# Selected attention: score products of the next unit issued in twos between the steps of a weight chunk

## The chip, the cores and the metric

The kernel runs on one core of one Trainium2 chip. The metric is the device time of one execution in microseconds; the kernel before takes 2013.05 us, the median of three runs (2012.48 to 2014.12).

## The reference, cut to what matters

The program is two transformer blocks on 512 tokens of width 1024, in float32. The first has a gated feed-forward, a windowed attention with a pooling branch and a second feed-forward. The second projects its input to the parts of a sparse attention (compressed keys, selected blocks, a window), of an RWKV-7 recurrence and of two gates, and ends with a convolutional feed-forward. The change touches the sparse attention:

```python
s_c = jnp.einsum('bsgrd,bcgd->bgrsc', q, kc).astype(jnp.float32) + bias_c
p_c = masked_softmax(s_c, dist_c >= 0, axis=-1)
o_cmp = jnp.einsum('bgrsc,bcgd->bsgrd', p_c, vc)
...
sc = jnp.einsum('bcgrd,bgcnld->bgrcnl', q_b, k_sel).astype(jnp.float32) + bias
p = masked_softmax(sc, mask, axis=(-2, -1))
...
o = gt[..., 0:1] * o_cmp + gt[..., 1:2] * o_slc + gt[..., 2:3] * o_win
```

There are 8 heads of width 64 in 2 groups of 4, and with 8 blocks of 64 keys every causal block is among the 16 selected, so selected and window attention are both causal attention over the keys up to the query, on keys of their own.

## The kernel before

The five engines each run a list of instructions written out by hand, joined by semaphores. All large weights come as one stream of chunks (128 x 1024 numbers). SP loads a chunk into one of 4 places of `w_raw`; POOL splits it into a high and a low float32r part (`split`, L445 and L447) when the chunk four earlier has been used (`w_used`); TensorE multiplies it. `chunk` (L521) does a chunk in 8 steps `k`, three 128x512 products each: `h_hi` by `w_hi` (L532), `h_lo` by `w_hi` (L533), `h_hi` by `w_lo` (L534), 24 in all, into one bank of PSUM.

The sparse attention is cut in 8 units (`units`): query tiles of 128 tokens, n = 0 to 3, by the two groups g. Unit 0 and 1 have n = 0, 2 and 3 n = 1, and so on. For a unit:

- TensorE, `nsa_scores` (L838): 10 score products into four banks in turn. Products 0 to 7 (L847) are one head each against the (n + 1) x 128 keys, on 64 rows of the array: even ones on rows 0 to 63, odd ones on rows 64 to 127. Products 8 and 9 (L854) are two heads each against the 8n + 7 compressed keys, again on one half of the rows each. Product i may overwrite its bank only when DVE has read product i - 4 (`nsa_masked`).
- DVE, `nsa_mask`: adds the bias to each product, writes it to `E` (L2000; `Ec`, L2008, for 8 and 9) and takes the minimum.
- ACT, `nsa_exps`: the exponential of each (L1458; for 8 and 9 two each, L1464), each with a read of its accumulator.
- DVE, `nsa_weights`: scales them by gate over sum (L2024 to L2036), then `nsa_weighed`.
- TensorE, `nsa_weigh` (L862): turns the weights 128 columns at a time (L880), ACT copies each turned item to `p2T` (L1479), TensorE multiplies it by the values (L894). Turned item x + 1 is issued ahead of the product of item x. ACT then copies the result to `oA` (L1483).

Between these, TensorE works through chunks of the RWKV and gate projections (`fill`, L759), one per unit; while the units run these go to bank 7, and ACT copies each to `stage` (L1404) when the chunk is used and sends it to memory (L1380). The orders of the three engines are, in TensorE's code,

```python
nsa_scores(*units[0], 0)
fill()
for u, (n, g) in enumerate(units):
    if u + 1 < len(units):
        nsa_scores(*units[u + 1], u + 1)
    fill()
    nsa_weigh(n, g, u)
```

on ACT `nsa_exps` of unit u + 1, then the copy of the chunk (`fill_out`), then the `p2T` copies of unit u; and on DVE `nsa_weights` of unit u, then `nsa_mask` of unit u + 1. All three work through their lists strictly in that order.

Of the kernel before, what the change touches and what calls it, by code (L numbers as in the profile page):

```python
# [115 lines left out]
def build(nc, x, positions, params, const, mix_const, w_pool, w_ffn1_gu, w_ffn1_down, w_in, w_out, w_ffn2_gu,  # L116
          w_ffn2_down, w_nsa, nsa_const, rel_bias, distance_code, cmp_pe, cmp_w1, cmp_w2,
          w_rwkv, rwkv_const, rwkv_w2a2, rwkv_g2, w_gates, w_merge, w_out_2, w_conv_up, w_conv_down, out):
    with ExitStack() as ctx:
# [5 lines left out]
        def sem(name):  # L125

            name = SHARED.get(name, (name, 0))[0]
            if name not in sems:
                sems[name] = ctx.enter_context(nc.semaphore(name))
            return sems[name]  # L130

        def nth(name, count):

            return sem(name), count + SHARED.get(name, (name, 0))[1]
# [34 lines left out]
        bank = [psum[:, i, :] for i in range(8)]  # L169
# [90 lines left out]
        def fill_bank(f):  # L260

            return 4 + f % 4 if f < 14 else 7 if f < NFILL - LATE else (0, 1, 2, 4, 5, 3, 0)[f - NFILL + LATE]
# [12 lines left out]
        def half_rows(x):  # L275
            return slice(C * x, C * x + C)
# [242 lines left out]
        @block.tensor  # L519
        def _(pe):  # L520
            def chunk(c, s, k0, k1, rhs_hi, rhs_lo, dst, start, stop, each=None, w0=None, also=None,  # L521
                      shift=0):


                w0 = k0 if w0 is None else w0
                pe.wait_ge(*nth("w_split", c + 1))
                for k in range(k0, k1):
                    if each:
                        pe.wait_ge(*nth(each, k + 1 + shift))
                    hi = w_hi[:, s, (k - w0) * P:(k - w0 + 1) * P]  # L530
                    lo = w_lo[:, s, (k - w0) * P:(k - w0 + 1) * P]
                    nc.tensor.matmul(dst, hi, rhs_hi[:, k, :], start=start and k == k0, stop=False)  # L532
                    nc.tensor.matmul(dst, hi, rhs_lo[:, k, :], start=False, stop=False)  # L533
                    last = nc.tensor.matmul(dst, lo, rhs_hi[:, k, :], start=False, stop=stop and k == k1 - 1)  # L534
                    if also:
                        also(k)
                return last
# [21 lines left out]
            def ffn_down(tag, c0, read):  # L559

                def body(i, first):
                    for u in range(4):
                        if not first:
                            pe.wait_ge(*nth(read, 4 * i + u - 3))
                        for j, (a, b) in enumerate(DOWN_SPLIT):
                            v = 3 * u + j
                            if first and u == 0:
                                pe.wait_ge(*nth(tag + "_a_ready", b))
                            last = chunk(12 * i + (c0 + v), (c0 + v) % RING, a, b, a_hi, a_lo, bank[4 + u][:, :],
                                         j == 0, j == 2)  # L570
                            last.then_inc(sem("w_used"), 1)
                body(0, True)
                body(1, False)
# [66 lines left out]
            for n in range(NT):  # L640
                pe.wait_ge(*nth(f"x_in{n}", 16))
                for k in range(KD):
                    last = nc.tensor.transpose(bank[k][:, n * P:(n + 1) * P], x_tok[:, n, k * P:(k + 1) * P], ident)
# [43 lines left out]
            for n in range(NT):  # L687
                last = nc.tensor.transpose(bank[6][:, n * P:(n + 1) * P], z[:, 1, n * P:(n + 1) * P], ident)
# [5 lines left out]
            units = [(n, g) for n in range(NT) for g in range(2)]  # L694
# [61 lines left out]

            filled = [0]

            def fill(n=1):  # L759

                for f in range(filled[0], filled[0] + n):
                    if f == NFILL - 1:
                        pe.wait_ge(*nth("fill_read", NFILL - LATE + 1))
                    elif 4 <= f <= NFILL - LATE:
                        pe.wait_ge(*nth("fill_read", f - 3 if f < 14 else f))
                    chunk(FIRST["rwkv"] + f, (FIRST["rwkv"] + f) % RING, 0, KD, h_hi, h_lo,
                          bank[fill_bank(f)][:, :], True, True).then_inc(sem("w_used"), 1)
                filled[0] += n

            pe.wait_ge(*nth("zn_read", 11))  # L770
            for v in range(2):
                b = job_bank()
                for n in range(NT):
                    last = nc.tensor.transpose(b[:, n * P:(n + 1) * P], zn[:, 2 + v, n * P:(n + 1) * P], ident)
# [13 lines left out]
            for n in range(NT):  # L788
                last = nc.tensor.transpose(b[:, n * 24:(n + 1) * 24], oA[0:24, 0, n * P:(n + 1) * P],
                                           ident[0:24, 0:24])  # L790
# [14 lines left out]
            for v in range(2):  # L805
# [3 lines left out]
                for h in range(2):  # L809
                    for j in range(16):  # L810
                        last = nc.tensor.matmul(b[:, h * 64:h * 64 + 2 * NCMP], cw1[:, j, h * P:(h + 1) * P],  # L811
                                                cmp_blocks[v][:, j, :, :], start=(j == 0), stop=(j == 15),
                                                skip_group_check=True)
# [4 lines left out]
                if v == 0:  # L818
                    for h in range(2):
                        last = nc.tensor.matmul(b[:, 0:2 * NCMP], cw2[:, 0, h, :], hid[:, h, 0:2 * NCMP],  # L820
                                                start=(h == 0), stop=(h == 1))
# [5 lines left out]
                else:  # L827
                    for g in range(2):
                        for h in range(2):
                            last = nc.tensor.matmul(b[0:NCMP, g * HD:(g + 1) * HD], hid[:, h, g * NCMP:(g + 1) * NCMP],  # L830
                                                    cw2[:, 1, h, 0:HD], start=(h == 0), stop=(h == 1),
                                                    skip_group_check=True)
# [2 lines left out]
            pe.wait_ge(*nth("nsa_read", 17))  # L835
            pe.wait_ge(*nth("kc_normed", 1))

            def nsa_scores(n, g, unit):  # L838


                for i in range(10):
                    b = bank[i % 4] if unit % 2 == 0 else bank[(i + 2) % 4]
                    if 10 * unit + i >= 4:
                        pe.wait_ge(*nth("nsa_masked", 10 * unit + i - 3))
                    if i < 8:
                        h, e = i % 4, i % 2
                        last = nc.tensor.matmul(b[:, 0:(n + 1) * P],  # L847
                                                qn[64 * e:64 * e + 64, 2 * g + h // 2, n * P:(n + 1) * P],
                                                kd[64 * e:64 * e + 64, 2 * (i // 4) + g, 0:(n + 1) * P],
                                                start=True, stop=True)  # L850
                    else:
                        e = i - 8
                        for h in range(2):
                            last = nc.tensor.matmul(b[:, h * 32:h * 32 + 8 * n + 7],  # L854
                                                    qn[64 * e:64 * e + 64, 2 * g + h, n * P:(n + 1) * P],
                                                    kcn[64 * e:64 * e + 64, g * NCMP:g * NCMP + 8 * n + 7],
                                                    start=(h == 0), stop=(h == 1), skip_group_check=True)
                    last.then_inc(sem("nsa_scores"), 1)
# [45 lines left out]
                turn[0] += len(items)  # L904

            units = [(n, g) for n in range(NT) for g in range(2)]
            nsa_scores(*units[0], 0)
            fill()
            for u, (n, g) in enumerate(units):
                if u + 1 < len(units):  # L910
                    nsa_scores(*units[u + 1], u + 1)
                fill()
                nsa_weigh(n, g, u)


# [140 lines left out]
            for m in range(4):  # L1056
# [33 lines left out]
                for half in range(2):  # L1090
                    pe.wait_ge(*nth(f"dt_ready{half}", 6 * m + 6))
                    pe.wait_ge(*nth("rw_tok", 4 * m + 4))
                    for i in range(2):
                        n = 2 * half + i
                        for e, c in DIAGONALS:
                            rows = half_rows(e)
                            last = nc.tensor.matmul(bank[HALF_BANKS[half][e]][half_rows(c), i * P:i * P + P],
                                                    DT[rows, 2 * n + c, :],
                                                    AtV[rows, n, c, :, :].rearrange("p a i -> p (a i)"), start=True,
                                                    stop=True, skip_group_check=True)  # L1100
                    last.then_inc(sem("ug"), 1)
                pe.wait_ge(*nth("ug_read", 2 * m + 2))
                for n in range(NT):
# [18 lines left out]
                    for qm, yn, tok, rows, e, ug in tiles:  # L1122
                        last = nc.tensor.matmul(yn[:, second], Kt[tok, n, rows], Vt[tok, n, rows], start=False,
                                                stop=True, skip_group_check=True)
# [4 lines left out]
            for c in range(1, NCH):  # L1129
# [4 lines left out]
                for e in range(2):  # L1134
                    rows = slice(64 * e, 64 * e + 64)
                    if c < NCH - 1:
                        for m in range(4):
                            last = nc.tensor.matmul(bank[2 + e][rows, m * HD:(m + 1) * HD], pin[rows, 4 + m, at],
                                                    state[rows, c % 2, m, :], start=True, stop=True,
                                                    skip_group_check=True)  # L1140
                        last.then_inc(sem("state_product"), 1)
                for e in range(2):
                    rows = slice(64 * e, 64 * e + 64)
                    for m in range(4):
                        last = nc.tensor.matmul(bank[e][rows, m * HD:(m + 1) * HD], state[rows, c % 2, m, :],
                                                pin[rows, m, at], start=True, stop=True, skip_group_check=True)
# [48 lines left out]
            for n in range(NT):  # L1195
                for h in range(2):
                    for k in range(4):
                        last = nc.tensor.transpose(bank[2 * n + h][:, k * P:(k + 1) * P],
                                                   xT[:, 4 * h + k, n * P:(n + 1) * P], ident)
# [1193 lines left out]
```

## Time and profile before

| | us |
|---|---|
| median of three runs | 2013.05 |
| lowest, highest | 2012.48, 2014.12 |
| the profiled execution, its own time | 2012.64 |
| its span in the profile | 2010.8 |
| TensorE busy (matrix products) | 1863.6 |
| POOL busy | 1278.4 |
| DVE busy | 836.7 |
| ACT busy | 426.4 |
| mean granted TensorE clock | 0.965 of 2.4 GHz |

The profile is of one execution. "Busy" is the time in which an engine had an instruction under way. The span is 1.84 us shorter than that execution's own time, which also holds what lies around the instructions.

### The profile page before, as it was taken

The numbers are of one execution on the slowest core, as the hardware profiler recorded it, in microseconds if no ns is written. First come the engines' busy times: TensorE is split into PE (matmuls) and PEld (weight loads), VectorE is DVE, ScalarE is ACT, GpSimd is POOL, SyncE is SP. The second block draws the span as 40 slices with busy tenths as digits, with TensorE's granted clock in tenths as the row PEclk, the third lists the DMA queues.
The fourth block names the chain that finished last, engine by engine and source line by source line (L and its number), as shares of the span: only waits on it lengthen the run. The fifth ranks groups of instructions, "written<-read, shape, count | busy, mean of one in ns | idle before, by whom it ended". The sixth has DMA issues, their size and how long they took to land.

```text
span 2010.8 us, 29786 instructions
## 1 busy us (share of the span) xinstructions
PE 1863.6 (93%) x11700; PEld 1480.8 (74%) x11700; DVE 836.7 (42%) x1399; ACT 426.4 (21%) x862; POOL 1278.4 (64%) x619
## 2 busy tenths in 40 slices
PE   6999999888779999999799999998868799999998
PEld 5888888656557888888487876676755678888887
DVE  4333321268654333311405344327657635555301
ACT  3000000122422000000213255535431022111100
POOL 6888888734076888888475542323355567777773
PEclk9999999889889999999899999999968899999999
DMA  4222233311021222233242431140023223322331
GB/s 152 94 95 102 93 93 95 118 37 58 11 84 64 103 95 94 89 98 106 98 162 85 158 131 53 43 152 9 4 112 115 68 81 102 95 94 93 95 97 61
DMA packets 58779, 180.32 MB, mean 90 GB/s; under 512 B 6931, under 2 KB 13843, under 8 KB 58172
## 3 DMA queue, kind: packets, MB, share of 16 engines
q1 hardware_dynamic: 49132, 165.83, 24.7%
q10 hardware_dynamic: 9552, 13.13, 1.9%
q8 instruction: 72, 1.18, 0.2%
q14 instruction: 23, 0.19, 0.0%
HBM read 165.81 MB, written 13.13 MB: 89 GB/s over the span
## 4 chain that ended last, share of the span: by engine, by line
PE 81%; DVE 12%; ACT 3%; issue 2%; DMA 0%; POOL 0%; ACTq 0%; SPq 0%; DVEq 0%; POOLq 0%
PE bank L532 23%; PE bank L533 23%; PE bank L534 23%; PE bank L894 1%; PE bank L847 1%; DVE h_lo L1660 1%; PE bank L582 1%; PE bank L880 1%; DVE sq L2223 1%; DVE m_lo L2224 1%; PE bank L811 1%; DVE xT L1707 1%; DVE tmp L1704 1%; PE bank L1052 1%; DVE sq L2220 1%
## 5 line engine op out<-in xcount | busy, mean ns | idle before, releaser
L445 POOL TENSOR_TENSOR w_hi<-w_raw,one 128x1024 fp32r<-128x1024 f32 (+1 forms) x279 | 527.4, 1890 | 554.1 <-PE bank L534 543.6
L447 POOL TENSOR_TENSOR w_lo<-w_raw,w_hi 128x1024 fp32r<-128x1024 f32 (+1 forms) x279 | 695.9, 2494 | 21.9
L532 PE MATMUL bank<-h_hi,w_hi 128*128 128x512 f32 x1528 | 619.7, 406 | 26.9 <-DVE h_lo L1660 12.6
L533 PE MATMUL bank<-h_lo,w_hi 128*128 128x512 f32 x1528 | 598.4, 392 | 0.0
L534 PE MATMUL bank<-h_hi,w_lo 128*128 128x512 f32 x1528 | 598.1, 391 | 0.0
L532 PEld LDWEIGHTS bank<-h_hi,w_hi 128*128 128x128 f32 x1528 | 289.0, 189 | 111.3 <-issue 29.0
L533 PEld LDWEIGHTS bank<-h_lo,w_hi 128*128 128x128 f32 x1528 | 289.1, 189 | 67.2 <-issue 9.9
L534 PEld LDWEIGHTS bank<-h_hi,w_lo 128*128 128x128 f32 x1528 | 288.8, 189 | 61.0
L532 PE MATMUL bank<-a_hi,w_hi 128*128 128x512 f32 x528 | 205.4, 389 | 0.0
L533 PE MATMUL bank<-a_lo,w_hi 128*128 128x512 f32 x528 | 205.4, 389 | 0.0
L534 PE MATMUL bank<-a_hi,w_lo 128*128 128x512 f32 x528 | 205.4, 389 | 0.0
L1255 ACT ACTIVATE tmp<-tmp 128x512 f32<-128x512 f32 x44 | 27.8, 632 | 426.6 <-DVE tmp L1671 426.6
L1697 DVE TENSOR_TENSOR acc<-acc,sq 128x512 f32<-128x512 f32 x16 | 30.5, 1907 | 207.8 <-ACT sq L1264 207.8
L532 PEld LDWEIGHTS bank<-a_hi,w_hi 128*128 128x128 f32 x528 | 99.1, 188 | 20.7
L534 PEld LDWEIGHTS bank<-a_hi,w_lo 128*128 128x128 f32 x528 | 99.1, 188 | 20.6
L533 PEld LDWEIGHTS bank<-a_lo,w_hi 128*128 128x128 f32 x528 | 99.1, 188 | 20.4
L1671 DVE TENSOR_TENSOR tmp<-bank,rstd 128x512 f32<-128x512 f32 x44 | 30.4, 691 | 132.5 <-PE bank L534 123.9
L1679 DVE TENSOR_TENSOR a_hi<-tmp,bank 128x512 f32 x44 | 30.3, 688 | 132.2 <-PE bank L534 132.2
L493 POOL TENSOR_TENSOR OT<-mats,rcs 128x256 f32<-128x256 f32 x40 | 32.5, 825 | 75.0 <-DVE mats L2132 62.2
L1633 ACT ACTIVATE tmp<-bank,prm 128x512 f32<-128x512 f32 x44 | 34.3, 779 | 147.8 <-DVE bank L2246 147.8
L1674 DVE TENSOR_TENSOR tmp<-tmp,rstd 128x512 f32<-128x512 f32 x44 | 47.2, 1072 | 31.4 <-ACT tmp L1255 31.4
L1264 ACT ACTIVATE sq<-bank 128x512 f32<-128x512 f32 x16 | 9.6, 598 | 229.7 <-PE bank L534 229.7
(342 smaller groups left out, 2088.4 us busy)
## 6 DMA issues: line engine op xcount, KB each, us to landing
w_raw<-w_ffn_gu_dram SPq DMA_DIRECT2D x88, 512.0 KB, 3.4
w_raw<-w_conv_up_dram SPq DMA_DIRECT2D x44, 512.0 KB, 3.5
w_raw<-w_ffn_down_dram SPq DMA_DIRECT2D x32, 448.0 KB, 3.2
w_raw<-w_ffn_down_dram SPq DMA_DIRECT2D x16, 512.0 KB, 3.5
w_raw<-w_out_dram SPq DMA_DIRECT2D x16, 512.0 KB, 3.5
w_raw<-w_gates_dram SPq DMA_DIRECT2D x16, 512.0 KB, 3.6
w_raw<-w_rwkv_dram SPq DMA_DIRECT2D x14, 512.0 KB, 3.5
w_raw<-w_conv_down_dram SPq DMA_DIRECT2D x16, 448.0 KB, 3.3
```

What stands on the lines that cost most here:

```text
L445: nc.gpsimd.tensor_tensor(w_hi[:, s, 0:width], raw, one[:, 0:1].to_broadcast([P, width]), ALU.mult).then_inc(sem("w_rounded"), 1)
L447: nc.gpsimd.tensor_tensor(w_lo[:, s, 0:width], raw, w_hi[:, s, 0:width].bitcast(F32), ALU.subtract).then_inc(sem("w_split"), 1)
L493: nc.gpsimd.tensor_tensor(OT[:, k % 2, units_of(half), :] .rearrange("p (n e) t -> p n e t", e=2), mats[:, 2 * half:2 * half + 2, :, 0, :] ...
L532: nc.tensor.matmul(dst, hi, rhs_hi[:, k, :], start=start and k == k0, stop=False)
L533: nc.tensor.matmul(dst, hi, rhs_lo[:, k, :], start=False, stop=False)
L534: last = nc.tensor.matmul(dst, lo, rhs_hi[:, k, :], start=False, stop=stop and k == k1 - 1)
L1255: nc.scalar.activation(tmp[:, u, :], tmp[:, u, :], ACT.Silu).then_inc(sem(tag + "_silu"), 1)
L1633: nc.scalar.activation(tmp[:, v, :], bank[2 * u + v][:, :], ACT.Identity, bias=bias, scale=w)\
L1671: nc.vector.tensor_tensor(tmp[:, u, :], bank[2 * u][:, :], rstd[:, :], ALU.mult)\
L1674: nc.vector.tensor_tensor(tmp[:, u, :], tmp[:, u, :], rstd[:, :], ALU.mult)\
L1679: nc.vector.tensor_tensor(hi, tmp[:, u, :], bank[2 * u + 1][:, :], ALU.mult)\
L1697: nc.vector.tensor_tensor(acc[:, :], acc[:, :], sq[:, m % 2, :], ALU.add).then_inc(sem(tag + "_acc"), 1)
```

## The change

`chunk` gets the option to increment `w_used` itself at its last product, ahead of what hangs behind the step. `nsa_scores` takes the list of products to do. Of each of the units 1 to 7, products 0 and 1 now stand ahead of the chunk, and products 2 and 3, 4 and 5, 6 and 7, 8 and 9 behind the chunk's steps k = 1, 3, 5 and 7. Unit 0 keeps its ten products ahead of a chunk. DVE's, ACT's, POOL's and SP's lists are the same as before. In the changed file TensorE's lines from L535 on stand two lines lower (L847 is L849, L854 is L856, L880 is L882, L894 is L896).

```diff
             def chunk(c, s, k0, k1, rhs_hi, rhs_lo, dst, start, stop, each=None, w0=None, also=None,
-                      shift=0):
+                      shift=0, count=False):
...
                     last = nc.tensor.matmul(dst, lo, rhs_hi[:, k, :], start=False, stop=stop and k == k1 - 1)
+                    if count and k == k1 - 1:
+                        last.then_inc(sem("w_used"), 1)
                     if also:
                         also(k)
                 return last
...
-            def fill(n=1):
+            def fill(n=1, also=None):
...
                     chunk(FIRST["rwkv"] + f, (FIRST["rwkv"] + f) % RING, 0, KD, h_hi, h_lo,
-                          bank[fill_bank(f)][:, :], True, True).then_inc(sem("w_used"), 1)
+                          bank[fill_bank(f)][:, :], True, True, also=also, count=True)
...
-            def nsa_scores(n, g, unit):
+            def nsa_scores(n, g, unit, some):
...
-                for i in range(10):
+                for i in some:
...
-            nsa_scores(*units[0], 0)
+            nsa_scores(*units[0], 0, range(10))
             fill()
             for u, (n, g) in enumerate(units):
                 if u + 1 < len(units):
-                    nsa_scores(*units[u + 1], u + 1)
-                fill()
+
+                    nsa_scores(*units[u + 1], u + 1, range(2))
+                    fill(also=lambda k: nsa_scores(*units[u + 1], u + 1, range(k + 1, k + 3) if k % 2 else ()))
+                else:
+                    fill()
                 nsa_weigh(n, g, u)
```

TensorE at unit 6 (n = 3), from the end of the unit before, in the kernel before:

```order
L894 MATMUL bank<-p2T,vct 64x128 [waits p2T_ready]
L894 MATMUL bank<-p2T,vct 64x128 x3
L847 MATMUL bank<-kd,qn 128x512 [waits masked] x8
L854 MATMUL bank<-kcn,qn 128x31 [waits masked]
L854 MATMUL bank<-kcn,qn 128x31
L854 MATMUL bank<-kcn,qn 128x31 [waits masked]
L854 MATMUL bank<-kcn,qn 128x31
L532 MATMUL bank<-h_hi,w_hi 128x512 [waits w_split,fill_read]
L533 MATMUL bank<-h_lo,w_hi 128x512
L534 MATMUL bank<-h_hi,w_lo 128x512
```

and in the changed kernel, as far as the second pair:

```order
L896 MATMUL bank<-p2T,vct 64x128 x3
L849 MATMUL bank<-kd,qn 128x512 [waits masked] x2
L532 MATMUL bank<-h_hi,w_hi 128x512 [waits w_split,fill_read]
L533 MATMUL bank<-h_lo,w_hi 128x512
L534 MATMUL bank<-h_hi,w_lo 128x512
L532 MATMUL bank<-h_hi,w_hi 128x512
L533 MATMUL bank<-h_lo,w_hi 128x512
L534 MATMUL bank<-h_hi,w_lo 128x512
L849 MATMUL bank<-kd,qn 128x512 [waits masked] x2
```

Here `kd,qn` are the eight score products; they stood in one run, and now stand two at a time with six products of the chunk between.

The end of the same chunk, where unit 5's weights are turned, in the changed kernel:

```order
L534 MATMUL bank<-h_hi,w_lo 128x512
L856 MATMUL bank<-kcn,qn 128x31 [waits masked]
L856 MATMUL bank<-kcn,qn 128x31
L856 MATMUL bank<-kcn,qn 128x31 [waits masked]
L856 MATMUL bank<-kcn,qn 128x31
L882 MATMUL bank<-ncs,E 128x128 [waits p2T_ready,nsa_weighed,out_read]
```

Before, L880 (now L882) followed L534 directly; the products with `kcn` (8 and 9) now stand between them.

ACT's list at the same place, the same in both kernels:

```order
L1463 ACTIVATE E,stat<-E,stat 128x512 [waits masked] x8
L1469 ACTIVATE Ec,stat<-Ec,stat 128x31 [waits masked]
L1469 ACTIVATE Ec,stat<-Ec,stat 128x31
L1469 ACTIVATE Ec,stat<-Ec,stat 128x31 [waits masked]
L1469 ACTIVATE Ec,stat<-Ec,stat 128x31
L1409 ACTIVATE stage<-bank 128x512 [waits fill_out1,w_used]
L1385 DMA rwkv_and_gates<-stage 128x512 [waits fill_read]
L1484 ACTIVATE p2T<-bank 128x512 [waits p2T_used,turned] x6
```

Nothing moved on ACT (its lines stand five lower in the changed file: L1458 is L1463, L1464 is L1469, L1404 is L1409, L1479 is L1484), but the products that its first twelve activations wait for have moved on TensorE.

## Rows read from the trace of the kernel before

**Rows 1.** The page: busy time, share of the span and instructions of each engine
```profile
PE 1863.6 (93%) x11700; PEld 1480.8 (74%) x11700; DVE 836.7 (42%) x1399; ACT 426.4 (21%) x862; POOL 1278.4 (64%) x619
```

**Rows 2.** Busy time by stretch, the eight units: stretch, us, engines, clock, DMA
```profile
1163.00:1295.00 132.00, 123.36 (x859) 90.56 (x859) 60.85 (x308) 76.69 (x247) 44.59 (x19) 1.00 0.21 67
```

**Rows 3.** Waits in 1163 to 1295: us in total, times, longest
```profile
PEld bank L847 <- DVE stat L2000: 9.1, 20, 1.3
...
PE bank L894 <- ACT p2T L1479: 6.0, 7, 0.9
```

**Rows 4.** Timeline of TensorE at unit 6: start us, us, instruction, count, idle before
```profile
1252.45 4.98 PE L847 MATMUL bank<-kd,qn 64*128 64x512 f32 x16
1256.92 1.24 PE L854 MATMUL bank<-kcn,qn 64*128 64x31 f32 x8
1258.09 0.50 PE L532 MATMUL bank<-h_hi,w_hi 128*128 128x512 f32 x1
1258.42 0.40 PE L533 MATMUL bank<-h_lo,w_hi 128*128 128x512 f32 x1
...
1263.43 0.39 PE L534 MATMUL bank<-h_hi,w_lo 128*128 128x512 f32 x1
1263.66 1.03 PE L880 MATMUL bank<-ncs,E 128*128 128x128 f32 x8
1265.57 0.66 PE L894 MATMUL bank<-p2T,v_tok 128*64 128x128 f32 x8 [0.87 <-ACT p2T L1479]
```

**Rows 5.** Timeline of TensorE's weight loads at unit 6
```profile
1252.45 0.30 PEld L847 LDWEIGHTS bank<-kd,qn 64*128 64x128 f32 x4 [0.17 <-issue]
1252.98 0.19 PEld L847 LDWEIGHTS bank<-kd,qn 64*128 64x128 f32 x2 [0.24 <-issue]
1253.41 0.19 PEld L847 LDWEIGHTS bank<-kd,qn 64*128 64x128 f32 x2 [0.24 <-issue]
1254.47 0.29 PEld L847 LDWEIGHTS bank<-kd,qn 64*128 64x128 f32 x2 [0.86 <-DVE stat L2000]
```

**Rows 6.** Timeline of DVE and ACT at unit 6
```profile
1253.72 0.69 DVE L2000 CUSTOM_DVE_ANT_0 E<-bank,toeplitz 128x512 f32<-128x512 f32 x1 [9.01 <-PE bank L847]
...
1258.61 0.20 DVE L2008 CUSTOM_DVE_ANT_0 Ec<-bank,toeplitz 128x31 f32<-128x31 f32 x1
...
1260.11 0.30 ACT L1464 ACTIVATE Ec<-Ec,stat 128x31 f32<-128x31 f32 x1
...
1261.23 0.18 ACT L1464 ACTIVATION_READ_ACCUMULATOR Ec<-Ec,stat 128x1 f32 x1
...
1263.86 0.60 ACT L1404 ACTIVATE stage<-bank 128x512 f32<-128x512 f32 x1 [2.44 <-PE bank L534]
...
1264.92 1.08 ACT L1479 ACTIVATE p2T<-bank 128x512 f32<-128x512 f32 x2 [0.46 <-PE bank L880]
```

**Rows 7.** Timeline of TensorE at units 1, 2 and 4 (n = 0, 1, 2)
```profile
1174.14 0.39 PE L534 MATMUL bank<-h_hi,w_lo 128*128 128x512 f32 x1
1174.45 0.72 PE L847 MATMUL bank<-kd,qn 64*128 64x128 f32 x8
...
1184.38 0.66 PE L894 MATMUL bank<-p2T,v_tok 128*64 128x128 f32 x8 [0.81 <-ACT p2T L1479]
...
1186.83 1.13 PE L847 MATMUL bank<-kd,qn 64*128 64x256 f32 x8
...
1197.92 0.66 PE L894 MATMUL bank<-p2T,v_tok 128*64 128x128 f32 x8 [0.87 <-ACT p2T L1479]
...
1216.26 4.02 PE L847 MATMUL bank<-kd,qn 64*128 64x384 f32 x16
...
1228.36 0.66 PE L894 MATMUL bank<-p2T,v_tok 128*64 128x128 f32 x8 [0.87 <-ACT p2T L1479]
```

**Rows 8.** Busy time by stretch in the first block's attention, columns as in group 2
```profile
500.00:510.00 10.00, 7.64 (x54) 5.61 (x52) 7.82 (x26) 4.42 (x14) 4.24 (x2) 1.00 0.14 52
...
518.00:525.00 7.00, 6.04 (x26) 3.31 (x26) 6.59 (x18) 3.10 (x12) 0.00 (x0) 0.51 0.01 2
```

## The prediction, made before the changed kernel ran

> **What bounds the kernel now.** I read the page first: TensorE is busy for 1863.6 of 2010.8 us [rows 1], so time is lost or won on TensorE's own list. Then the busy time of the stretch that the change touches, the eight units of the sparse attention: 132 us, TensorE busy 123.36, ACT 76.69, DVE 60.85, POOL 44.59, clock 1.00 [rows 2]. POOL works for a third of it, so the weight chunks are ready and splitting them is no limit here. Then the waits there: TensorE's loads for the score products wait 9.1 us in 20 waits for DVE, which must empty a bank before the fifth and later products may overwrite it, and the first product of the weights with the values (L894) waits 6.0 us in 7 waits for ACT's copy to `p2T` [rows 3]. The change goes at the first of these. Then the timelines of one unit, the scores of unit 6, engine by engine, since what a moved product costs depends on who waits for it.
>
> What the reader is to see in TensorE's timeline [rows 4]: the ten products take from 1252.45 to 1258.09, 5.64 us; the chunk's 24 products follow, the last at 1263.43; the turned weights at 1263.66; and then TensorE stands until 1265.57, when the first `p2T` copy is there. From score product 0 to that L894 it is 13.12 us. In the same way it is 9.93 for n = 0, 11.09 for n = 1, 12.10 for n = 2 [rows 7]. What follows L894 (copies and products in turn, then the next unit) is not changed, so this distance is what the change moves, seven times.
>
> The loads [rows 5] show how score products run: four loads at once (two passes each of products 0 and 1, which sit on different halves of the rows), then two loads every 0.43 us. Each product is two passes, the halves run side by side, the first pass takes 0.53 and a following one 0.43. Product 4's loads come at 1254.47, after 0.86 us of waiting for DVE.
>
> **The change part by part.** *Removed:* the wait for DVE, since each pair of products now has a chunk step pair of some 1.4 us between it and the next, and DVE needs about 0.6 for a mask. The last products of a unit (8 and 9) also go side by side instead of one after the other.
>
> *Added on TensorE:* a change between whole-row and half-row products, twice for every pair. Going in: after a chunk product the next comes 0.23 later (22 intervals from 1258.42 to 1263.43), but the score product came 0.31 after L534 [rows 4, 7]: 0.09 more. Going out: the last small pass of L854 starts about 0.20 before L532 (end of the group 1258.16, less 0.27 for one pass), some 0.13 more than its columns need, and L533 comes 0.33 after L532 instead of 0.23 [rows 4]: together 0.24. A pair between steps of the chunk then costs 0.09 + 0.53 + 0.43 + 0.24 = 1.29 us for 512 columns, where a pair in a run costs 0.86.
>
> The Trainium skill (TensorEngine Tiling, Key Properties) says that changing the tiling mode, as opposed to the tile, drains the engine; these rows agree, with 0.09 and 0.24 us. Another page of it (TensorE: Matmul & The Clock Gate, "What happens when you issue a matmul") has the load of the next stationary operand pulled ahead of running products where it goes to the background buffer; by that rule alone the way in would cost nothing, and the sum below would be 0.09 x 4 x 7 = 2.5 us less. The row of the late load speaks against it.
>
> *Moved, and who waits:* this is the term that decides. ACT works in order: twelve exponentials of the next unit, the copy of the chunk, the `p2T` copies. Before, the exponentials were over at 1261.41 (the accumulator read at 1261.23 and its 0.18) and ACT then waited 2.44 us for the chunk's end; the copy of the chunk began at 1263.86 [rows 6]. Now products 8 and 9 run only when the chunk is over, so their masks and their four exponentials stand between the chunk's end and ACT's copies, while TensorE, after turning two items, has nothing to do.
>
> The walk for n = 3, from score product 0: products 0 and 1 take 0.53 + 0.43, and L532 comes 0.13 later, at 1.09. From L532 to the last L534 it is 5.34 [rows 4] plus three inserted pairs of 1.29: 10.30. Masks and the first eight exponentials keep up: a pair comes every 2.7 us, and ACT takes about 0.71 for each. Behind the last L534: 0.31 to the load of product 8, 0.36 for its first three of four passes, 0.31 to DVE (1253.72 less 1252.98 and 0.43 [rows 5, 6]), 0.36 for two small masks and the signal (estimate: two at some 0.13, an accumulator read, 0.05), 1.25 for four exponentials (1260.11 to 1261.41, the last read overlapping the next by some 0.05 to 0.1), 1.06 from the copy of the chunk to `p2T`, which holds the issue of a DMA, and 0.65 from there to L894 [rows 4, 6]. That is 4.30, so L894 at 14.6 against 13.12: **1.5 us later**. TensorE itself would have been ready about 2.4 us sooner, where it waited 0.87 before. So what the pairs save on TensorE is lost in this wait.
>
> For fewer columns only the eight passes ahead of the last L534 shrink, to 0.32 and 0.21 by their share of 512 columns, and for 128 columns to about 0.09 (an estimate below that share's 0.11, so that n = 0 is not overstated). L894 then comes at 13.7, 12.9 and 11.7 (for n = 0 I take 0.1 off for small masks and exponentials of 7 columns): 1.6, 1.8 and 1.8 later than before. Units 1 to 7 are one of n = 0 and two each of the others: 1.8 + 2 x 1.8 + 2 x 1.6 + 2 x 1.5 = **11.6 us**. Unit 0 keeps its order, and unit 7's weights are turned behind a chunk without scores. DVE's weights of a unit end about 4.4 us after its exponentials, around 17.4 for n = 3, while the next scores start near 21.8 (1272.73 before is 7.16 after L894): covered. The earlier count of `w_used` costs nothing: ACT reaches the copy later anyway, and POOL has slack. Nothing behind the stage is released by anything but this chain, so I pass the 11.6 us on whole. Against the profiled execution's 2012.64 that is 2024.2; the median of the runs lies 0.4 above it, so 2024.6.
>
> Bounds. If changing between whole and half rows is free, the walk is shorter by 4 x 0.09 + 3 x 0.24 = 1.08 per unit, and only 4.0 us are added: 2017. If the two products of a pair do not run side by side when they are alone (as the late ones before, started one by one), each pair costs one pass more: 4 x (0.1 + 2 x 0.21 + 2 x 0.32 + 2 x 0.43) = 8.1 us, 2033. I take the middle, since products 0 and 1 of unit 1 did start together right behind a chunk [rows 7] and the two switches are measured.
>
> **The rivals.** *The scores' wait was what counted (faster).* If the last exponentials are not what ACT's copies wait for, TensorE gains the waits for DVE and the parallel products 8 and 9. With free switches the block of 5.64 us shrinks to 3.54 for eight products and about 0.65 for the rest, 1.45 less for n = 3; in the same way 1.3, 1.1 and 0.9 for smaller n, 8.7 us together: 2004.4. For it: 9.1 us of waits [rows 3]. Against: it decides only if ACT is done with the exponentials before the chunk's last product, and they are put behind it. Chance 0.03.
>
> *The switches eat the gain and ACT stays hidden (no change).* TensorE's own list, without the wait: L880 would come at 10.30 + 0.31 + 0.36 + 0.18 = 11.15 for n = 3, against 11.21 before, and some 0.1 to 0.3 later than before for smaller n, about 1 us in all: 2014.1. It needs the four exponentials and the copy to fit under the turning, 1.03 us, which their 1.25 alone exceeds. Chance 0.05.
>
> *The clock falls (slower still).* Waits of 2.4 us in each unit could let the granted clock fall from 2.4 to 1.2 GHz. In the first attention it stayed at 1.00 with TensorE busy for 7.64 of 10 us, and was at 0.51 in a stretch soon after [rows 8]; here TensorE stays busy for some 85%. One stretch of 3.4 us at half clock per unit would cost 1.7 x 7 = 12 us more: 2036.6. The skill's page on the clock gate says idle stretches bring this; the first of the two rows speaks for no fall here. Chance 0.03.
>
> *Single pairs don't overlap*, 2033 as above: chance 0.05.
>
> **How the numbers follow.** The forecast has 0.84. About 0.2%, 4 us, is what a measurement of this kernel can tell from no change. Slower by more: 0.84 + 0.03 + 0.05 = 0.92; the same 0.05; faster 0.03. The range runs from just above the lower bound, 2018, to 2031, short of the upper: the terms of the walk behind the chunk may each be 0.1 to 0.2 off in all seven units, some 3 us, and the price of a switch as much.
>
> **What would show it.** In the profile of the changed kernel: the loads' waits for DVE fall from 9.1 to under 2 us; the waits of L894 for ACT rise from 6.0 to about 17; ACT's copy of the chunk no longer waits for L534 but follows the last exponential at once; two score products start together behind each second step, and the chunk's next product comes about 1.3 us later than without them for 512 columns; the stretch of the units is 144 us instead of 132, clock 1.00. It would be wrong if L894 waited less than 1.5 us per unit, or if work behind the units took the delay up.

## The result, and the profile after

The changed kernel takes 2031.88 us (median of four runs, 2027.96 to 2034.31) against 2012.76 for the kernel before (2007.68 to 2014.12, four runs of which three are those above): a ratio of 1.0097, with a 95% interval of 1.0080 to 1.0113. A second set on one chip gave 2028.43 against 2011.98, ratio 1.0083 (1.0056 to 1.0110). So it is slower, as forecast, by 16 to 19 us where 12 had been forecast; 2031.88 lies 0.9 above the range.

The page of the changed kernel, first group of numbers (answers to [rows 1]):

```profile
PE 1870.4 (92%) x11700; PEld 1474.0 (73%) x11700; DVE 849.7 (42%) x1399; ACT 428.6 (21%) x862; POOL 1273.3 (63%) x619
```

The same 11700 products are under way for 6.8 us longer. To compare the place itself, here is the busy time from the first score product of unit 1 to the last product of unit 7's weights with the values, in the kernel before (columns as in [rows 2]):

```profile
1174.45:1312.17 137.72, 129.25 (x936) 94.46 (x936) 55.35 (x270) 76.63 (x232) 43.96 (x18) 1.00 0.17 55
```

and in the changed kernel:

```profile
1171.17:1328.71 157.54, 140.45 (x937) 90.63 (x936) 68.23 (x270) 78.90 (x232) 38.24 (x18) 0.94 0.14 48
```

The stretch grew by 19.8 us, and its clock is no longer 1.00. All of the growth is here: the rest of the span went from 1873.1 to 1868.6 us, with less half clock (a granted clock of 0.50, 1.2 GHz) in it. The first two falls of the clock, in the changed kernel:

```profile
1185.70:1199.00 13.30, 11.13 (x67) 7.20 (x65) 6.52 (x31) 7.60 (x28) 4.19 (x2) 1.00 0.13 51
1199.00:1205.80 6.80, 6.80 (x32) 4.13 (x30) 3.60 (x17) 2.06 (x6) 0.06 (x1) 0.50 0.35 118
...
1216.10:1222.90 6.80, 6.43 (x38) 4.24 (x40) 3.79 (x13) 2.11 (x5) 1.02 (x1) 0.50 0.35 116
```

There are two more such stretches, of 3.4 us, from 1257.0 and from 1301.4: some 20.5 us at 1.2 GHz in all, where the kernel before had none in its units. Each begins between 0.4 us before and 1.0 us after the end of one of the waits for `p2T`. Those waits, in 1163 to 1310 (answers to [rows 3]):

```profile
PEld bank L849 <- DVE stat L2005: 4.2, 9, 1.3
...
PE bank L896 <- ACT p2T L1484: 15.4, 7, 2.3
```

The waits for DVE went from 9.1 to 4.2 us, those for ACT's `p2T` copy from 6.0 to 15.4. Unit 6 in TensorE's timeline (answers to [rows 4]):

```profile
1264.68 1.13 PE L849 MATMUL bank<-kd,qn 64*128 64x512 f32 x4
1265.74 0.50 PE L532 MATMUL bank<-h_hi,w_hi 128*128 128x512 f32 x1
1266.54 0.40 PE L532 MATMUL bank<-h_hi,w_hi 128*128 128x512 f32 x1
...
1267.32 1.13 PE L849 MATMUL bank<-kd,qn 64*128 64x512 f32 x4
1268.38 0.50 PE L532 MATMUL bank<-h_hi,w_hi 128*128 128x512 f32 x1
...
1274.93 0.39 PE L534 MATMUL bank<-h_hi,w_lo 128*128 128x512 f32 x1
1275.25 0.64 PE L856 MATMUL bank<-kcn,qn 64*128 64x31 f32 x8
1275.83 1.09 PE L882 MATMUL bank<-ncs,E 128*128 128x128 f32 x8
1279.19 0.66 PE L896 MATMUL bank<-p2T,v_tok 128*64 128x128 f32 x8 [2.27 <-ACT p2T L1484]
```

and in ACT's (answers to [rows 6]):

```profile
1275.23 0.71 ACT L1463 ACTIVATE E<-E,stat 128x512 f32<-128x512 f32 x1
1276.28 0.32 ACT L1469 ACTIVATE Ec<-Ec,stat 128x31 f32<-128x31 f32 x1 [0.26 <-DVE stat L2013]
...
1277.51 0.57 ACT L1409 ACTIVATE stage<-bank 128x512 f32<-128x512 f32 x1
1278.12 0.33 ACTq L1385 DMA_DIRECT2D rwkv_and_gates<-stage  x1
1278.54 1.08 ACT L1484 ACTIVATE p2T<-bank 128x512 f32<-128x512 f32 x2 [0.46 <-ACT stage L1409]
```

From score product 0 to the first L896 it is 14.51 us, 14.6 by the prediction's walk. The last L534 comes at 10.25 (10.30 by the walk). A pair between the steps puts 1.84 us between two starts of L532 (1266.54 to 1268.38) where 0.68 is usual, and what follows that L532 comes 0.12 late: a pair costs 1.28 us against the forecast's 1.29. ACT's copy of the chunk no longer waits for the chunk, but for the four small exponentials ahead of it.

### The profile page after: what moved, and what is told of

The parts are those of the page before. It is cut to its first block, busy times and chain, and to the rows that moved or that the text cites. A ratio compares the mean times of both kernels' runs of the same rounds, so it can differ in the third digit from the quotient of the medians.

```text
span 2026.2 us, 29786 instructions
## 1 busy us (share of the span) xinstructions
PE 1870.4 (92%) x11700; PEld 1474.0 (73%) x11700; DVE 849.7 (42%) x1399; ACT 428.6 (21%) x862; POOL 1273.3 (63%) x619
## 4 chain that ended last, share of the span: by engine, by line
PE 82%; DVE 12%; ACT 3%; issue 2%; DMA 0%; POOL 0%; ACTq 0%; SPq 0%; DVEq 0%; POOLq 0%
PE bank L532 24%; PE bank L534 23%; PE bank L533 23%; PE bank L896 1%; PE bank L849 1%; DVE h_lo L1665 1%; PE bank L882 1%; PE bank L584 1%; DVE xT L1712 1%; DVE tmp L1709 1%; PE bank L813 1%; PE bank L1057 1%; DVE win L1804 1%; DVE sc L1832 0%; DVE sq L2228 0%
## 5 line engine op out<-in xcount | busy, mean ns | idle before, releaser
L445 POOL TENSOR_TENSOR w_hi<-w_raw,one 128x1024 fp32r<-128x1024 f32 (+1 forms) x279 | 522.1, 1871 | 576.3 <-PE bank L534 565.4
L532 PE MATMUL bank<-h_hi,w_hi 128*128 128x512 f32 x1528 | 621.6, 407 | 27.4 <-DVE h_lo L1665 12.4
L534 PE MATMUL bank<-h_hi,w_lo 128*128 128x512 f32 x1528 | 598.1, 391 | 0.0
L532 PEld LDWEIGHTS bank<-h_hi,w_hi 128*128 128x128 f32 x1528 | 288.5, 189 | 123.5 <-issue 41.7
L534 PEld LDWEIGHTS bank<-h_hi,w_lo 128*128 128x128 f32 x1528 | 288.8, 189 | 61.1
L532 PE MATMUL bank<-a_hi,w_hi 128*128 128x512 f32 x528 | 205.4, 389 | 0.0
L534 PE MATMUL bank<-a_hi,w_lo 128*128 128x512 f32 x528 | 205.4, 389 | 0.0
L532 PEld LDWEIGHTS bank<-a_hi,w_hi 128*128 128x128 f32 x528 | 99.1, 188 | 20.8
L534 PEld LDWEIGHTS bank<-a_hi,w_lo 128*128 128x128 f32 x528 | 99.1, 188 | 20.4
```

The source lines that it names most:

```text
L445: nc.gpsimd.tensor_tensor(w_hi[:, s, 0:width], raw, one[:, 0:1].to_broadcast([P, width]), ALU.mult).then_inc(sem("w_rounded"), 1)
```

## The experiments

Theory A: ACT's exponentials of products 8 and 9 behind the chunk's end hold its copies up, and TensorE's longer standing still lets the clock fall. Theory B: the changes between half and whole rows are the cost. tail_only, act_order, kept_busy and early_tail ran in one set with the kernel before (2011.99, 19 runs); kept_half, two_blocks, two_blocks_copy_late and after_again ran in the second set (2011.98, 17 runs), on the same chip; copy_late_alone came last (2011.1, 12 runs). All edits are against the changed kernel, except that copy_late_alone changes the kernel before.

**tail_only.** Of the change, only products 8 and 9 behind the last step:

```diff
-                    nsa_scores(*units[u + 1], u + 1, range(2))
-                    fill(also=lambda k: nsa_scores(*units[u + 1], u + 1, range(k + 1, k + 3) if k % 2 else ()))
+                    nsa_scores(*units[u + 1], u + 1, range(8))
+                    fill(also=lambda k: nsa_scores(*units[u + 1], u + 1, range(8, 10) if k == 7 else ()))
```

> Products 0 to 7 of the next unit in one run ahead of the chunk, as before; only 8 and 9 stand behind the chunk's last step. Theory A (ACT's four small exponentials behind the chunk's end hold up its copies, and TensorE's wait then lets the clock fall): L894 waits about 2.1 us per unit, 15 us in all, as in the changed kernel; the walk gives the last L534 at 10.3 us for n = 3 (10.3 there too), some 0.2 earlier for n = 0 and 1; at full clock 10.5 us over before, with half-clock stretches in the units 2023 to 2032. Theory B (the four changes between half and whole rows in each unit are the cost): three of the four are gone, L894's wait is no price, so 7 us or more come back: 2024 or below, near 2015 without the last one.

Measured: 2029.5 us, ratio 1.0090 (1.0068 to 1.0112). That is 17.5 us above before, within what theory A expected. Busy time from unit 1 to unit 7, then unit 6 in TensorE's timeline:

```profile
1174.54:1331.00 156.46, 139.16 (x936) 97.80 (x936) 66.87 (x270) 76.60 (x232) 38.22 (x18) 0.92 0.14 48
```

```profile
1266.94 4.98 PE L849 MATMUL bank<-kd,qn 64*128 64x512 f32 x16
1277.52 0.64 PE L856 MATMUL bank<-kcn,qn 64*128 64x31 f32 x8
1278.09 1.09 PE L882 MATMUL bank<-ncs,E 128*128 128x128 f32 x8
1281.46 0.66 PE L896 MATMUL bank<-p2T,v_tok 128*64 128x128 f32 x8 [2.28 <-ACT p2T L1484]
```

It is 14.52 us from product 0 to L896, 14.51 in the changed kernel: taking three of the four pairs out of the chunk gave nothing back at n = 3, because the run of eight then waits for DVE again (8.8 us in all). L896's waits are 15.4 us as in the changed kernel, and the clock fell five times. The last pair alone makes almost all of the loss. Theory B, by which 7 us or more would have come back, is refuted.

**act_order.** TensorE's list as changed, on ACT the four exponentials behind the second `p2T` copy:

```diff
+                    if after and x == 1:
+                        after()
...
-                    nsa_exps(*units[u + 1], u + 1)
-                fill_out()
-                nsa_copies(n, g, u)
+                    nsa_exps(*units[u + 1], u + 1, range(8))
+                    fill_out()
+                    nsa_copies(n, g, u, lambda: nsa_exps(*units[u + 1], u + 1, (8, 9)))
+                else:
+                    fill_out()
+                    nsa_copies(n, g, u)
```

> The changed kernel's TensorE list untouched; on ACT the four exponentials of products 8 and 9 stand behind the second p2T copy instead of ahead of the copy of the chunk. Theory A: L894 is back near its old distance (about 13.1 us for n = 3), its waits near 6 us in all, the third p2T copy comes up to 0.5 us late; no or few half-clock stretches in the units: 2015, between 2012 and 2018. Theory B: TensorE's list is the same, so the time is the changed kernel's less 2 us at most: 2029.

Measured: 2009.33 us, ratio 0.9995 (0.9983 to 1.0008): no change from before, and below theory A's 2012 to 2018. Busy time, and ACT at unit 6:

```profile
1172.90:1309.72 136.82, 131.67 (x936) 85.32 (x936) 58.23 (x270) 77.36 (x232) 38.27 (x18) 1.00 0.17 55
```

```profile
1261.58 0.57 ACT L1409 ACTIVATE stage<-bank 128x512 f32<-128x512 f32 x1
...
1262.61 1.09 ACT L1484 ACTIVATE p2T<-bank 128x512 f32<-128x512 f32 x2 [0.45 <-PE bank L882]
1263.58 0.32 ACT L1469 ACTIVATE Ec<-Ec,stat 128x31 f32<-128x31 f32 x1
...
1264.80 0.58 ACT L1484 ACTIVATE p2T<-bank 128x512 f32<-128x512 f32 x1
```

With TensorE's list untouched the whole loss is gone: 136.82 us for the stretch, 0.9 less than before, and the clock at 1.00. The distance to L896 is 12.94 us for n = 3 and 10.77 for n = 1, below the 13.12 and 11.09 of before. The third copy starts 2.19 us behind the first (before 1.93), so it is 0.26 late, not 0.5. So the position of four activations on ACT is the cause. The changes between half and whole rows are not free, though: L896 now waits 4.3 us for ACT in 1163 to 1310, where it waited 6.9 before, and the stretch is only 0.9 us shorter. Without that gain the stretch would be some 1.7 us longer than before (an estimate, late third copies included), so the changes cost a little more than the removed waits for DVE gave.

**kept_busy** and **kept_half.** The changed kernel, with eight (kept_busy, shown here) or four (kept_half) products that nobody reads in TensorE's wait:

```diff
                     if x + 1 < len(items):
                         turn_item(x + 1)
+                    if x == 0 and unit + 1 < NUNIT:
+                        pe.wait_ge(*nth("nsa_masked", 10 * (unit + 1) + 8))
+                        b = bank[2] if unit % 2 else bank[0]
+                        for _ in range(8):
+                            nc.tensor.matmul(b[:, :], h_hi[:, 1, 0:P], h_hi[:, 0, :], start=True, stop=True)
```

> The changed kernel with eight products more in each of units 0 to 6, of data that nobody reads, written to a bank that is free, while TensorE waits for the first p2T copy. They take 1.8 us of a wait of 2.1 to 2.3. If the wait lets the clock fall: no half-clock stretch is left in the units, and the time is the walk's, 12 us over before: 2024 to 2026, some 6 to 8 below the changed kernel. If the half-clock stretches there come from something else: they stay, and the time is the changed kernel's, 2031, or up to 1 us more.

> The changed kernel with four products more in each wait (0.9 us) instead of eight (1.8 us), so that TensorE stands still for 1.2 to 1.4 us per unit, between the kernel before (0.87) and the changed one (2.1 to 2.3). If the length of standing still is what the clock goes by: fewer half-clock stretches in the units than in the changed kernel, none to two, and 2024 to 2028. If eight products helped by something else than filling the wait: as many stretches as in the changed kernel, 2031.

Measured: 2025.94 us with eight, ratio 1.0062 (1.0040 to 1.0085); with four, in the second set, 2026.77, ratio 1.0066 (1.0040 to 1.0092). Busy time with eight:

```profile
1174.03:1322.99 148.96, 144.58 (x992) 95.09 (x992) 68.36 (x270) 78.93 (x232) 38.46 (x18) 1.00 0.15 50
```

and with four, with the wait of one unit in TensorE's timeline:

```profile
1173.02:1321.98 148.96, 138.16 (x964) 89.83 (x964) 67.93 (x268) 78.93 (x232) 38.30 (x18) 1.00 0.16 50
```

```profile
1271.42 1.17 PE L909 MATMUL bank<-h_hi 128*128 128x512 f32 x4
1273.94 0.66 PE L896 MATMUL bank<-p2T,v_tok 128*64 128x128 f32 x8 [1.36 <-ACT p2T L1489]
```

More work in the same waits, and the stretch is 8.6 us shorter than the changed kernel's, with the clock at 1.00. L896 comes where it came (14.53 us for n = 3), so nothing but the clock was won. Both give 148.96: with waits of 1.14 to 1.36 us the clock stayed at 1.00 in this stretch, and with 2.07 to 2.28 it fell after some of them. 148.96 less the 137.72 of before is 11.2 us, the walk's share.

The whole times bear this out less sharply. In the second set kept_half is 1.7 us below the changed kernel (2026.77 against 2028.43, four runs each), kept_busy 5.9 below the first set's changed kernel, and the intervals of the ratios overlap. Both kept kernels are 14 to 15 us above the kernel before, of which the stretch explains 11.2. So the 8.6 us hold for the stretch in the profiled executions; what the clock is worth in the median is not measured to better than several microseconds.

The wait's length is not the whole rule. Unit 0, which lies ahead of this stretch and which the change leaves alone, has a wait of 1.12 us in all profiles. In three of eleven (kept_half, early_tail and copy_late_alone) the clock fell for 3.4 us, some 2.3 to 2.4 us after the wait's end. Here is kept_half, TensorE's timeline and then the busy time:

```profile
1164.10 1.12 PE L849 MATMUL bank<-kd,qn 64*128 64x128 f32 x8 [1.12 <-DVE stat L2010]
```

```profile
1166.46:1169.87 3.41, 3.41 (x9) 2.64 (x9) 1.04 (x7) 2.23 (x14) 0.30 (x1) 0.50 0.65 197
```

What brought these three falls was not tested. Nor do the two kept runs tell the length of a single wait from the share of time that TensorE stands still: they shorten both.

**early_tail.** Products 0 to 3 ahead, the pairs behind steps 1, 3 and 5:

```diff
+                    nsa_scores(*units[u + 1], u + 1, range(4))
+                    fill(also=lambda k: nsa_scores(*units[u + 1], u + 1, range(k + 3, k + 5) if k in (1, 3, 5) else ()))
```

> Products 0 to 3 ahead of the chunk, 4 and 5, 6 and 7, 8 and 9 behind steps 1, 3 and 5; nothing behind step 7. As many changes between half and whole rows as in the tail of the changed kernel less one. Theory A: the exponentials are over when the chunk ends, L894's wait is back at about 6 us in all, no half-clock stretch in the units, and TensorE's own list is 0.4 us shorter than before for n = 3, 0.26 for n = 2, 0.1 for n = 1: 1.5 us faster than before, 2011. Theory B: three pairs with changes cost about 1 us per unit over the run: 2018 to 2020.

Measured: 2012.73 us, ratio 1.0002 (0.9988 to 1.0016), which can't tell theory A's 2011 from no change, but rules out theory B's 2018 to 2020. The waits for ACT are as expected, and so is the clock in units 1 to 7, but the stretch is 138.38 us, 0.7 longer than before and not 1.5 shorter. The distances to L896 are 0.2 and 0.35 below before for n = 2 and 3, 0.3 above for n = 0, and 0.6 and 0.8 above for n = 1. DVE at unit 2, and POOL there:

```profile
1184.91 1.73 DVE L2031 TENSOR_TENSOR stat<-stat,gate_tok 128x12 f32<-128x12 f32 x1
1186.68 2.39 DVE L2035 TENSOR_SCALAR stat<-stat,prm 128x4 f32<-128x4 f32 x1
...
1191.22 0.41 DVE L2005 CUSTOM_DVE_ANT_0 E<-bank,toeplitz 128x256 f32<-128x256 f32 x1
```

```profile
1184.73 1.89 POOL L445 TENSOR_TENSOR w_hi<-w_raw,one 128x1024 fp32r<-128x1024 f32 x1 [4.14 <-PE bank L534]
1186.70 2.35 POOL L447 TENSOR_TENSOR w_lo<-w_raw,w_hi 128x1024 fp32r<-128x1024 f32 x1
```

Two tiny DVE instructions end when POOL's two do. The masks of unit 2 therefore begin 2.4 us behind its first score product (1188.78) instead of 0.85, and the loads of products 4 and 5 wait 0.62 us for them in the middle of the chunk.

**two_blocks**, **two_blocks_copy_late** and **copy_late_alone.** From the theory, a shorter order: products 4 to 7 in one run behind step 1, 8 and 9 behind step 3; and ACT's copy of the chunk behind the second `p2T` copy, with that order and with the order of before.

```diff
+                    nsa_scores(*units[u + 1], u + 1, range(4))
+                    fill(also=lambda k: nsa_scores(*units[u + 1], u + 1,
+                                                   range(4, 8) if k == 1 else range(8, 10) if k == 3 else ()))
```

```diff
+                    if x == 1:
+                        after()
...
-                fill_out()
-                nsa_copies(n, g, u)
+                nsa_copies(n, g, u, fill_out)
```

> Products 0 to 3 ahead of the chunk, 4 to 7 in one run behind step 1, 8 and 9 behind step 3. Two changes into half rows inside the chunk instead of four, the exponentials over before the chunk is. By the walk with the measured prices TensorE's list is shorter than before by 0.8 us for n = 3, 0.65 for n = 2, 0.5 for n = 1, 0.3 for n = 0: 4.2 us in all, less some waits for the masks of products 0 to 3: 2008 to 2010. If changes between half and whole rows cost more than the 0.3 us per pair that the walk takes, the kernel is no faster than before: 2012 or more.

> The same, and on ACT the copy of the chunk stands behind the second p2T copy instead of ahead of the first. L894's wait of 0.87 us, which the copy and its DMA issue make, goes; the third p2T copy comes some 0.2 late: 0.65 us in each of 8 units, 5 us less than without it, 2003 to 2005. If ACT's copy was not what L894 waited for in the kernel before, it is as without it: 2008.

> The kernel before, with ACT's copy of the chunk behind the second p2T copy and nothing else changed. In the kernel with two blocks this edit shortened the distance from the first score product to L894 by 0.6 us per unit, 4.2 us over units 1 to 7. If that wait is made by the copy and its DMA issue, whatever the order on TensorE, the distances are 9.3, 10.5, 11.5 and 12.5 us (0.6 less than before) and the stretch of the units 4.2 us shorter: 2007 to 2009. If it depended on the score products standing in two blocks: no change, 2012.

Measured: 2008.09 us (ratio 0.9976, 0.9962 to 0.9990) for two blocks; 2000.66 (0.9942, 0.9922 to 0.9962) with the late copy, both against 2011.98; and 2007.8 against 2011.1 (0.9984, 0.9972 to 0.9997) for the late copy alone. The first and the last lie in their expected ranges; the two together are faster than the expected 2003 to 2005. The stretches are 133.93, 129.73 and 133.22 us; here that of two blocks, then of the two together:

```profile
1172.77:1306.70 133.93, 126.28 (x936) 87.27 (x936) 80.91 (x270) 77.86 (x232) 39.84 (x18) 1.00 0.17 56
```

```profile
1173.42:1303.15 129.73, 126.67 (x935) 87.60 (x936) 80.93 (x270) 76.88 (x232) 39.81 (x18) 1.00 0.18 58
```

In the stretch it is 3.8 us from the blocks (4.2 expected), 4.5 from the copy (4.2), and 8.0 from both: they add up there. The medians give 3.9, 3.3 and 11.3 us, each uncertain by 2.5 to 4. ACT at unit 6 with both:

```profile
1255.99 0.31 ACT L1470 ACTIVATE Ec<-Ec,stat 128x31 f32<-128x31 f32 x1
1257.91 1.08 ACT L1485 ACTIVATE p2T<-bank 128x512 f32<-128x512 f32 x2 [1.52 <-PE bank L882]
1258.88 0.61 ACT L1410 ACTIVATE stage<-bank 128x512 f32<-128x512 f32 x1
```

ACT is now idle for 1.52 us ahead of the `p2T` copy, waiting for TensorE's turned weights, and TensorE's own wait at L896 is down to 0.25 us. This kernel beats the one before by 0.6% and the changed one of the same set by 1.4%.

**after_again.** The changed kernel in the second set:

> The changed kernel once more, for its spread and to stand beside the kernels of this set: 2027 to 2034, with three to six half-clock stretches inside the units and none of them in the kernel before.

Measured: 2028.43 us. The clock fell five times within the units, for 20.5 us in all, in a stretch of 157.69 us. The first profile of the changed kernel had four falls with the same sum.

## Why the prediction was right or wrong

- *ACT's copies behind the last exponentials decide*: right, shown by act_order. L894's (now L896's) wait was forecast at 2.4 us per unit, about 17 in all; it is 2.07 to 2.28, 15.4 in all.
- *The walk*: right. From product 0 to L896, for n = 0 to 3, the forecast was 11.7, 12.9, 13.7 and 14.6 us; measured 12.09, 12.70, 13.6 and 14.5. In n = 0 the chunk's first product also waited 0.27 us for ACT's copy of the chunk before, which the walk had not. The sum at full clock, 11.2 us, was forecast at 11.6.
- *Price of a pair*: 1.28 against 1.29. With the four exponentials out of the way (act_order) TensorE's side came out some 1.7 us longer than before by the estimate above, near the 1 us of the rival "the switches eat the gain". The bounds "switches free" and "pairs don't overlap" were both away from the truth.
- *DVE's waits gone*: mostly; 4.2 us were left and not under 2 as forecast; unit 0, which is not changed, has 1.3 of them in one wait. Nothing hung on it.
- **The step that failed is the rival "the clock falls"**, which was given 0.03 and put at nothing in the forecast's sum. It is no rival but a consequence of the very wait that the forecast computed. Over units 1 to 7 it cost 8.6 us by two profiles (157.54 and 157.69 against 148.96); the medians of the whole kernels differ by 1.7 to 5.9 us. The rival's 12 us had been for 3.4 us at half clock in each of seven units, 23.8 us of it; measured were 20.5 us. The forecast of 2024.6 with these 8.6 us is 2033.2, against 2031.88; without a fall in units 1 to 7 kept_busy took 2025.94, so the rest of the sum was near.

I had argued the fall away with a share, a stretch at full clock in which TensorE was busy for 7.64 of 10 us [rows 8]. But in the changed kernel it was busy for 11.13 of 13.30 us, a higher share, and the clock fell at the end of it. The trace of the kernel before had a closer case. Just ahead of the stretch that I cited and in it, no fall followed single waits of 2.06 and 1.90 us; the next as long, of 2.48 us, was followed by one at 518.1. And 1.1 us after a wait of 2.58 us in another stage the clock fell, although TensorE had been busy for 12.52 of 15.10 us. Three of these waits in TensorE's timeline, then the busy time around the last:

```profile
494.75 1.15 PE L633 MATMUL bank<-pT,v_tok 128*64 128x128 f32 x16 [2.06 <-ACT pT L1314]
...
516.46 1.09 PE L624 MATMUL bank<-cst,sc 128*128 128x128 f32 x8 [2.48 <-DVE sc L1847]
...
970.97 1.13 PE L742 MATMUL bank<-acc,cst 128*128 128x512 f32 x2 [2.58 <-DVE acc L1697]
```

```profile
957.00:972.10 15.10, 12.52 (x53) 9.39 (x51) 1.85 (x1) 1.08 (x2) 13.35 (x7) 1.00 0.11 32
972.10:978.90 6.80, 3.19 (x4) 1.41 (x5) 5.25 (x8) 3.21 (x5) 1.02 (x1) 0.50 0.92 288
```

The forecast wait of 2.4 us lies between 2.06 and 2.48, so the rows of before left a fall open and did not speak against it. That single waits matter more than the share is my reading of these rows; no run held the share and changed the waits.

- *The sign* was right, slower by more than 0.2%, and for the reason given: ACT's late copies.

## What to carry to other kernels

Work that another engine's in-order list waits for must not be moved behind the event which that list's next step needs anyway: here two small products behind a chunk's last step put four activations of 0.3 us between the chunk and the copies that TensorE stands waiting for. Where an edit makes TensorE stand still longer in one piece, compute both prices, the wait and the slower products after it. A high busy share is no evidence that the clock will hold: here it fell after 11.13 busy of 13.30 us. A cheap test tells the two prices apart: fill the wait with products that nobody reads, and see what comes back in that stretch.

## What was not expected of the hardware

In units 1 to 7 the clock fell only around waits of 2.07 to 2.28 us, and not always: at four of seven in the changed kernel's profile, at five of seven in after_again and in tail_only. No fall there went with waits of 1.36 us or less. Unit 0 is the exception told under kept_half: a wait of 1.12 us, and a fall after it in three of eleven profiles. So the same kernel can have a different number of slow stretches from one execution to the next.

A DVE instruction on 128 x 12 numbers takes 0.17 us in all eight units of the kernel before, and 1.85 us here, where POOL splits a chunk beside it. In the changed kernel's timeline of DVE:

```profile
1277.90 1.85 DVE L2031 TENSOR_TENSOR stat<-stat,gate_tok 128x12 f32<-128x12 f32 x1
```

and of POOL:

```profile
1277.38 2.35 POOL L447 TENSOR_TENSOR w_lo<-w_raw,w_hi 128x1024 fp32r<-128x1024 f32 x1
```

The two end within 0.02 us of each other. DVE's busy time over the stretch rose from 55.35 to 68.23 us, most of it in this one line (its median is 1.91 us in the changed kernel), and to 80 us in early_tail and 81 in two_blocks. The Trainium skill (SBUF — State Buffer, "Who interferes with whom") says that DVE and GpSimd (POOL) share a pair of ports, and that a DVE instruction with two SBUF inputs contends with a GpSimd instruction that reads SBUF. L2031 has two such inputs, and these rows agree. In early_tail the two units of n = 1, whose masks came late, took 1.4 us more than before, which is most of the gap between the 1.5 us expected and no gain. That POOL is the cause is read from ends that coincide; moving POOL's splits against DVE's scaling was not tried.
